# A two-block transformer on one core: squares of the pre-MLP norm added on VectorE, a third slot for split weights, and the last PSUM copies on ScalarE

## The reference, cut to what matters

```python
for l in range(DEPTH):                     # DEPTH = 2, D = 1024, D_FF = 4096, all float32
    h = rms_norm_2(x, pre_mix_w[l])
    u = h @ w_in[l]                        # in2_l
    ...                                    # convolution, attention, gated delta rule
    y = concat([y_conv, y_diff, y_delta]) @ w_out[l]          # out2_l
    x = x + rms_norm_2(y, post_mix_w[l])   # post-norm and
    h = rms_norm_2(x, pre_mlp_w[l])        # pre-norm, both at the start of ff1_l
    y = square(relu(h @ w_ff1[l])) @ w_ff2[l]                 # ff1_l, ff2_l
    x = x + rms_norm_2(y, post_mlp_w[l])
# rms_norm_2(x, w) = x * rsqrt(mean(x*x, over the 1024 channels) + 1e-6) * w
```

## Time and profile before

| what | value |
|---|---|
| median of 3 runs | 4168.87 us (4166.24 to 4171.51) |
| profiled execution, its own time | 4178.81 us |
| its span | 4177.0 us |
| PE busy | 3878.9 us, 93% |
| DVE busy | 2185.2 us, 52% |
| ACT busy | 1493.1 us, 36% |
| POOL busy | 343.9 us, 8% |

### The profile page before, as it was taken

The page is one execution under the profiler, slowest core; times in us unless marked ns, Lnnn a source line. Parts: engine busy times, 40 slices in busy tenths (PEclk is TensorE's granted clock), DMA queues, the critical chain, the costliest instruction groups (busy, mean ns, idle before and its releaser), DMA issues. The chain is left out here.

```text
span 4177.0 us, 49727 instructions
## 1 busy us (share of the span) xinstructions
PE 3878.9 (93%) x20585; PEld 3108.8 (74%) x20585; DVE 2185.2 (52%) x3124; ACT 1493.1 (36%) x2290; POOL 343.9 (8%) x296
## 2 busy tenths in 40 slices
PE   7997789999999999889999979989998979988998
PEld 4884667888888777678877757757786757866876
DVE  5725755555564332373256756543475846544375
ACT  2115632111453112152255335433364335533264
POOL 0000210000000000000000034300000025400000
PEclk9998989999999999999999979979999979988999
DMA  5510013343222111122323100022232200012231
GB/s 201 174 33 10 6 41 101 111 141 111 66 66 74 58 58 51 38 91 91 100 83 99 57 11 1 1 81 71 90 101 67 81 11 1 1 61 71 91 101 60
DMA packets 254720, 288.90 MB, mean 69 GB/s; under 512 B 6756, under 2 KB 226939, under 8 KB 254517
## 3 DMA queue, kind: packets, MB, share of 16 engines
q1 hardware_dynamic: 252437, 281.84, 20.9%
q10 hardware_dynamic: 2080, 4.19, 0.3%
HBM read 283.92 MB, written 2.10 MB: 68 GB/s over the span
## 5 line engine op out<-in xcount | busy, mean ns | idle before, releaser
L465 PE MATMUL banks<-h_halves,w_halves 128*128 128x512 f32 (+1 forms) x3728 | 1393.6, 374 | 60.0 <-DVE h_halves L259 42.3
L466 PE MATMUL banks<-h_halves,w_halves 128*128 128x512 f32 (+1 forms) x3728 | 1389.0, 373 | 0.0
L467 PE MATMUL banks<-h_halves,w_halves 128*128 128x512 f32 (+1 forms) x3728 | 1382.7, 371 | 0.0
L465 PEld LDWEIGHTS banks<-h_halves,w_halves 128*128 128x128 f32 x3728 | 714.9, 192 | 201.4 <-issue 49.1
L467 PEld LDWEIGHTS banks<-h_halves,w_halves 128*128 128x128 f32 x3728 | 712.4, 191 | 122.7
L466 PEld LDWEIGHTS banks<-h_halves,w_halves 128*128 128x128 f32 x3728 | 714.6, 192 | 118.4 <-issue 0.5
L259 DVE TENSOR_TENSOR w_halves<-work,w_halves 128x2048 fp32r<-128x2048 f32 (+1 forms) x215 | 488.3, 2271 | 466.5 <-ACT w_halves L254 466.3
L254 ACT ACTIVATE w_halves<-work 128x2048 fp32r<-128x2048 f32 (+1 forms) x215 | 407.3, 1894 | 524.8 <-PE banks L467 388.5
L254 ACT ACTIVATE h_halves<-kept 128x512 fp32r<-128x512 f32 (+1 forms) x520 | 332.3, 666 | 313.2 <-PE banks L467 234.0
L259 DVE TENSOR_TENSOR h_halves<-kept,h_halves 128x512 fp32r<-128x512 f32 (+1 forms) x520 | 361.4, 737 | 137.5 <-ACT h_halves L254 136.8
L990 DVE SCALAR_TENSOR_TENSOR kept<-kept 128x512 f32<-128x512 f32 x280 | 188.3, 746 | 7.4 <-DMA kept<-in_mod_w 7.4
(11 more groups left out here) (372 smaller groups left out, 4759.9 us busy)
## 6 DMA issues: line engine op xcount, KB each, us to landing
work<-in_w_ff SPq DMA_DIRECT2D x64, 1024.0 KB, 5.3
work<-in_ffn_w_in SPq DMA_DIRECT2D x44, 1024.0 KB, 5.1
kept<-in_mod_w SPq DMA_DIRECT2D x40, 1024.0 KB, 5.1
work<-in_odd_w_in SPq DMA_DIRECT2D x24, 1024.0 KB, 5.2
work<-in_w_in SPq DMA_DIRECT2D x24, 1024.0 KB, 5.0
work<-in_ffn_w_out SPq DMA_DIRECT2D x16, 1024.0 KB, 5.2
work<-in_even_w_in SPq DMA_DIRECT2D x13, 1024.0 KB, 5.2
work<-in_odd_w_out SPq DMA_DIRECT2D x8, 1024.0 KB, 5.3
```

The source lines that it names most:

```text
L465: nc.tensor.matmul(o, low[:, k - a, fc], rh[:, tc], start=(k == 0), stop=False)
L466: nc.tensor.matmul(o, high[:, k - a, fc], rl[:, tc], start=False, stop=False)
L467: mm = nc.tensor.matmul(o, high[:, k - a, fc], rh[:, tc], start=False, stop=(k == K - 1))
```

## The change

1. `PlainNorm` with `post`: the squares of x are no longer summed on TensorE tile by tile. `add_square` adds them on VectorE into `home.total`, each one behind the next tile's low half, and one set of `row_sums` (`squares_complete`) stands before the last tile of group 1.
2. A third pair of halves, `t_halves`. Where `third` is set (`up`, that is `ff1_l`, and `following`, that is `in2_1`) the stage before also splits unit 1, into it; the stage itself starts with two units split, and group 1 of the pair reads `t_halves`. The split of unit 1 in the norm is gone.
3. `CopySum`: in the last group ScalarE squares both banks and then copies both; VectorE only adds.

```diff
@@ PlainNorm
-        if self.post and g == 0:
-            for t in ([k - 1] if k else []) + ([k] if k == KD - 1 else []):
-                pe.wait_ge(self.squared, t + 1)
-                self.home.row_sums(self.nc, 7, self.home.sq[t % 2], t == 0, t == KD - 1).then_inc(self.sq_used, 1)
+    def squares_complete(self, pe):
+        pe.wait_ge(self.sq_used, KD)
+        self.home.row_sums(self.nc, 7, self.home.total).then_inc(self.summed, 1)
...
+    def add_square(self, dve, k):
+        if k == 0:
+            return
+        dve.wait_ge(self.squared, k + 1)
+        if k > 1:
+            dve.wait_ge(self.sq_used, k)
+        total = self.home.total
+        self.nc.vector.tensor_tensor(total, total if k > 1 else self.home.sq[0], self.home.sq[k % 2],
+                                     ALU.add).then_inc(self.sq_used, 1 if k > 1 else 2)
...
                 if k:
                     self.lower(dve, k - 1)
+                    self.add_square(dve, k - 1)
             self.lower(dve, KD - 1)
+            self.add_square(dve, KD - 1)
@@ Dense.run, two_groups
+                        if k == K + lag - 1:
+                            before.squares_complete(pe)
                         if k >= lag:
                             group_tile(1, k - lag)
-                    before.behind_groups(pe)
+                    before.back(pe)
@@ Dense.run, splitter
                 if self.started:
-                    eng.sem_inc(halves_done, 1)
+                    eng.sem_inc(halves_done, self.started)
...
-                    second(eng, (lambda: weights(0, 1)) if paired else None)
+                    second(eng)
...
-                if units > 1 and not paired:
+                if units > 1 and self.started < 2:
                     weights(0, 1)
@@ Dense.run, next_halves of ScalarE (VectorE's is alike)
                     after.first_high(act).then_inc(next_high, 1)
+                    if after.third:
+                        if fly:
+                            act.wait_ge(rhs_low, (G * C - 1) * KD)
+                        after.first_high(act, 1).then_inc(next_high, 1)
@@ CopySum
+            if n == KD - 2:
+                self.held = banks[0]
+            if n == KD - 1:
+                for m, bank in enumerate((self.held, banks[0])):
+                    nc.scalar.activation(core.sb(where(g, m) + CTX, SEQ), bank, ACT.Copy).then_inc(free, 1)
...
-            dve.wait_ge(self.sq_done, 2 * g + f + 1)
-            nc.vector.tensor_copy(core.sb(where(g, f) + CTX, SEQ), banks[0]).then_inc(free, 1)
+            if 2 * g + f < KD - 2:
+                dve.wait_ge(self.sq_done, 2 * g + f + 1)
+                nc.vector.tensor_copy(core.sb(where(g, f) + CTX, SEQ), banks[0]).then_inc(free, 1)
```

More of the change, by code:

```diff
@@ L278, in __init__ @@
         self.widths = widths or {}
-        self.base, self.retired, self.started = None, False, False
+        self.base, self.retired, self.started, self.third = None, False, 0, False
     def width(self, g):
@@ L299, in preload, with place, first_high, first_low @@
             self.load(sp, 0, u)
[L301 to L308, removed]
+    def place(self, u, low):
+        if u == 1 and self.third:
+            return self.core.t_halves[:, low * SLOT_W:(low + 1) * SLOT_W]
+        return self.core.half(u % SLOTS, low)
+    def first_high(self, act, u=0):
+        act.wait_ge(self.core.ring_ready[u], self.base[u] + 16)
+        self.started = u + 1
+        return halves_high(self.core, act, self.place(u, 0), self.core.sb(RING0 + u * SLOT_W, SLOT_W))
+    def first_low(self, dve, u=0):
+        return halves_low(self.core, dve, self.place(u, 1), self.core.sb(RING0 + u * SLOT_W, SLOT_W), self.place(u, 0))
     def run(self, name, after=None, before=None, side=None):
@@ L481, in group_tile @@
                         pe.wait_ge(low_done, j + 1)
-                    high, low = (core.half(j, n).rearrange("p (k n) -> p k n", k=KD) for n in range(2))
+                    high, low = (self.place(j, n).rearrange("p (k n) -> p k n", k=KD) for n in range(2))
                     if j == 0:
@@ L599, in next_halves @@
                     after.first_low(dve)
+                    if after.third:
+                        dve.wait_ge(next_high, 2)
+                        after.first_low(dve, 1)
                 first, second = (before.vector_first, before.vector) if before is not None else (None, None)
@@ L1133, in tensor, with scalar @@
         self.home.spread(self.nc, 0, places).then_inc(self.spread, 1)
-    def scalar(self, act, weights=None):
+    def scalar(self, act):
         core, nc = self.core, self.nc
@@ L1158, in lower, with vector @@
         ins.then_inc(self.low, 1)
-    def vector(self, dve, weights=None):
+    def vector(self, dve):
         core, nc = self.core, self.nc
@@ L1237, in after_tile, with back, scalar @@
     def after_tile(self, pe, g, k):
-        if self.post and g == 0:
-            for t in ([k - 1] if k else []) + ([k] if k == KD - 1 else []):
-                pe.wait_ge(self.squared, t + 1)
-                self.home.row_sums(self.nc, 7, self.home.sq[t % 2], t == 0, t == KD - 1).then_inc(self.sq_used, 1)
         if not self.post and (g, k) == (0, 4):
-            self.behind_groups(pe)
-    def behind_groups(self, pe):
+            self.back(pe)
+    def squares_complete(self, pe):
+        pe.wait_ge(self.sq_used, KD)
+        self.home.row_sums(self.nc, 7, self.home.total).then_inc(self.summed, 1)
+    def back(self, pe):
         pe.wait_ge(self.rstd_done, 1)
         self.home.spread(self.nc, 1, self.places(6)).then_inc(self.spread, 1)
-    def scalar(self, act, weights=None):
+    def scalar(self, act):
         core, nc = self.core, self.nc
@@ L1254, in scalar @@
             self.home.root(nc, 0, 5).then_inc(self.y_std, 1)
-            weights()
         for k in range(KD):
@@ L1268, in scalar @@
         if self.post:
-            act.wait_ge(self.sq_used, KD)
+            act.wait_ge(self.summed, 1)
             self.home.root(nc, 1, 7).then_inc(self.std_done, 1)
@@ L3408, in second_layer @@
     up = Dense(core, a["w_ff1_2"][l], core.h, KD, D_FF // GW, plain(0), lat, ScaledSquaredRelu(core, nc, U0))
+    up.third = True
     out.run(f"out2_{l}", after=up)
@@ L3413, in second_layer @@
                                                     (PV0 + ROW_POSTMIX + 8 * l, y_view)))
+    if following is not None:
+        following.third = True
     down.run(f"ff2_{l}", after=following)
```

1 line of the change is left out of this document (added).

## The result

The changed kernel takes 4139.42 us (median of 4 runs, 4136.52 to 4142.80), the kernel before 4167.56 (4 runs, 4165.21 to 4171.51): ratio 0.9927, 95% interval 0.9913 to 0.9941, or 28.1 us faster by the medians (30.4 by the ratio). The forecast was 4143.7, with a range of its own of 4139 to 4148.

A forecast was written before the change was run, and what follows sets the result against it. TensorE, 93% busy, was taken to bound the kernel. Per stage 0.91 + 1.0 + 8.2 - 1.9 - 0.15 = 8.06 us; three stages 24.2, plus 1.0 at the end: 4168.87 - 25.2 = 4143.7, own range 4139 to 4148, wider 4137 to 4152.

The forecast's parts named there:

- Third slot: Post-norm start of three stages: unit 1's split moves to the stage before, first y product sooner, gain 0.91 us a stage.
- Its cover: End of the stage before: the added split should finish before the last group's squares, 3.2 us ahead on VectorE in out2_0.
- Copies: End of all four CopySum stages: ScalarE copies both banks, VectorE only adds; gain 1.0 us each, bounds 0.4 to 1.2.
- Squares: Inside the pair: TensorE loses seven of eight sets of narrow row sums, gain 8.2 us a stage.
- Given back: Between the pair and group 2: later row sums delay the weights' split; 1.9 us a stage lost, TensorE idle about 4 us.
- Does VectorE keep up: Inside the pair: seven more VectorE adds, blocked by GpSimd's three, deliver just in time; charge 0.15 us a stage, bounds 0 and 3.
- the layout: Step-by-step VectorE schedule inside the pair, with GpSimd's blocking: when low halves arrive against when TensorE wants them.
- Restart: Start of group 2: TensorE already restarts at the low clock, so its longer idle is charged nothing more.
- Rival 2: Both starts of each stage: higher clock 6 products sooner without interrupting row sums, 2.4 us a stage more, 4136.5; 1 in 12.
- Rival 1: Inside the pair: VectorE starves TensorE, which waits 2 to 3 us a stage, 4151; 1 in 10.
- Rival 3: Inside the pair: short waits for low halves keep the clock at 1.2 GHz, 16.8 us a stage, 4194; 1 in 25.
- Rival 4: Stage before: unit 1's load lands late, squares queue behind its split, 1 to 2 us a stage lost, 4148; 1 in 14.

The follow-up runs named there:

- squares: The kernel before with only the squares added on VectorE and one set of row sums: 4149.28 us, ratio 0.9955.
- load: The changed kernel with a second, useless VectorE add of 0.60 us behind each added square: 4147.54 us, ratio 0.9961 to the kernel before.
- again: The kernel before, unchanged, run as a control: 4167.72 us, ratio 1.0004.
- early: The changed kernel with the row sums two tiles sooner and the spread ahead of the last tile: 4125.02 us, ratio 0.9890 to the kernel before.
- slot: The kernel before with only the third pair of halves, unit 1 split in the stage before: 4156.72 us, ratio 0.9970.
- shift1: The kernel before with a useless VectorE add of 128 x 3584 at the start of in2_0, outside the changed stages: 4171.36 us, ratio 1.0014.
- copies: The kernel before with only the last two CopySum copies moved to ScalarE: 4155.28 us, ratio 0.9967.
- border: The kernel before with the third pair of halves and ScalarE's copies together, squares still on TensorE: 4157.64 us, ratio 0.9974.
- earlynopool: The kernel early with GpSimd's three adds to x given to VectorE: 4129.21 us, ratio 0.9903 to the kernel before.
- nopool: The changed kernel with GpSimd's three adds to x given to VectorE: 4143.14 us, ratio 0.9936 to the kernel before.
- hold: The kernel early with a useless VectorE add between the spread and its copy, lengthening TensorE's idle: 4138.22 us, ratio 0.9929 to the kernel before.

## Why the prediction was right, and where it was short

The mechanism held, and the time lies inside the forecast's own range, 0.4 us above its lower end. Its terms for a stage, against the traces (means of three; the unchanged kernel's two profiled executions agree within 0.1 but for D):

- *Third slot*, 0.91: measured 0.90, alone and in the whole. Its cover held: between split and first square ScalarE idled 5.9, 6.6 and 5.9 us.
- *Copies*, 1.0: measured 1.01 to 1.02.
- *Squares*, 8.2: B fell by 8.50. Some 8.2 are the seven sets. The rest comes from the clock: 11, 8 and 11 products of the three pairs run slowly, where 12 each did, at 0.2 us a product. In the kernel squares B fell by 8.0, with 14, 13 and 12 slow ones.
- *Given back*, 1.9: measured 1.80. TensorE's idle there is 3.9 us, as said.
- *Does VectorE keep up*, 0.15: measured 0 in two stages and 0.2 in `in2_1`. VectorE itself waited 0.34 us ahead of low halves 3 and 5 (not 5 in `in2_1`), since ScalarE waits there for GpSimd's x. In `ff1_0` the low halves 3, 5 and 6 ended 0.6, 0.8 and 0.8 us before the first product that uses them, where the layout had 0.4, 0.1 and 0.1. load shows how near this is: 0.60 us a tile more, and TensorE waits 1.8 us a stage.
- *Restart*, charged 0, "so I charge nothing more for that": D is 13.28 and not 13.83 us (13.36 in again, where one stage was slow for a shorter time). Of group 2's first products 14, 13 and 14 ran slowly before and 11, 9 and 11 now. The clock is low for the same 6.83 us; before, then now, in `ff1_0`:

```profile
2849.98:2856.81 6.83, 6.17 (x15) 0.50 0.38 131
2832.75:2839.58 6.83, 5.14 (x12) 0.50 0.48 154
```

  Group 2 starts at 2850.64, 0.66 us into the stretch, and now at 2834.44, 1.69 us into it: more of it passes while TensorE waits. What the term left out is larger: with a shorter wait there is no low stretch at all (early, 11.01).
- *Not in the sum*: the row sums of y take 1.48, 1.03 and 1.48 us for 1.86, and so root and spread come sooner: 0.4 us in two stages, 0.8 in `in2_1`. They start 1.0 us sooner, and in `ff1_0` the clock falls only 0.44 us after their start, where it had fallen 0.74 us before it. The 0.8 is in part luck of the execution: slot, squares and shift1, whose row sums start no sooner, also took 1.03 in `in2_1`, and copies 1.68.

So a stage gains 9.7 us by these rows and not 8.06 (64.94 - 55.25), the final one 28.4 - 27.1 = 1.3: 30.4 in all. The two profiled executions differ by 42.0. The other 11.6 lie outside what the change touches, and again, the same kernel, shows what they are: its profiled execution took 4168.88 and not 4178.81, 6.5 of these 9.9 us before the first changed stage. Against it the four parts give 3 x 9.25 + 1.0 = 28.7, and the medians 28.1. The prediction was right to set its sum against the medians.

Rival 2 (more through the clock, 4136.5) had the right effect at too large a price, some 1.0 to 1.4 us a stage and not 2.4, and the wrong cause: in squares, where the row sums are gone too, no fewer products ran slowly. Rival 1: 0.60 us a tile more brings it on; how much less would do wasn't run, and tile 5 of `in2_1` already shows its first sign. Rival 3 has nothing for it: waits inside the pair left the clock high. Rival 4 had 5.9 us of room on ScalarE.

**Why the parts do not add.** The pair starts at the low clock, so a microsecond taken out ahead of it has no fixed price. Here is the stretch at 1.2 GHz around the pair's start in `ff1_0` (us, PE busy, PEclk, DMA share, GB/s): before, squares, copies, slot, border, after.

```profile
2802.19:2819.26 17.07, 9.80 (x31) 0.50 0.41 123
2795.85:2812.92 17.07, 10.04 (x30) 0.50 0.40 123
2799.09:2812.74 13.65, 7.12 (x24) 0.50 0.50 154
2793.26:2806.92 13.66, 7.46 (x24) 0.50 0.49 154
2797.56:2811.21 13.65, 8.02 (x26) 0.50 0.48 154
2795.21:2808.86 13.65, 8.02 (x26) 0.50 0.48 154
```

Counted from the first square, it ends at 19.8 us before and at 20.1 in squares, and at 16.6 in copies, in slot, in border and after (in `in2_1`, in the same order: 19.0, 18.8, 16.4, 15.5, 15.4, 15.1). In `ff1_0` either part alone ends it 3.2 us sooner, and the second adds nothing to that: it lets products start sooner that then run at half speed (slow products of the three pairs: 12, 12, 12 before, 9, 8, 6 in copies, 8, 7, 7 in slot, 12, 9, 12 in border). From the first square to the pair's last product (A + B) it is 47.53 us before, 45.40 with copies, 45.33 with slot, 44.64 with both: the first microsecond brings 2.2, the second 0.7. D goes the same way: 13.8 and 13.4 before, 12.1 and 12.6 with one part, 12.8 with both. In the whole, the border's two parts on top of squares bring 58.22 - 55.25 = 3.0 us a stage, 8.9 in three, and 0.9 at the end; the medians say 9.9.

Against again, a stage gains 3.4 us by copies, 3.0 by slot and 6.3 by squares, 12.7 in sum, and 9.25 in the whole. Copies and slot each claim some 2 us a stage of the clock beyond their own 1.0 and 0.9; the whole keeps 1.0. So the sum of 46.8 is too large by 3.4 us a stage, 10.2 of its 18.7, because it counts a share that comes only once. Squares has next to none of that share. The other 8.5 us show in no row of these stages and lie within what the times leave open.

The Trainium skill's page "SBUF — State Buffer", section "Who interferes with whom", was used as the reason for the charge at GpSimd's adds. The trace agrees that the two exclude each other for whole instructions: the first low half again took 1.67 us. But who waits is not always VectorE: at tiles 3 and 5 it was GpSimd in five of six cases (2.33 us for 1.26), at no cost to TensorE, and VectorE in the sixth (1.78 us for 0.68), where TensorE lost 0.2 us. The charge laid out by that rule was due in one stage of three.

**What stays open.** The rows of the three stages and the end give 11.2 us for copies (3 x 3.42 + 0.95) and 14.1 were measured; for slot 8.9 and 12.6; for border 11.4, and 10.0. What is left, 1 to 4 us of either sign, is within the intervals, and lies in stretches that these kernels leave alone; those took 3939 to 3954 us in the profiled executions. Why the low stretch around the pair's start ends some 3 us sooner with either part isn't shown, only that it does. Why a 2.1 us idle slows the restart in 19 of the 21 stages looked at and not in two, and 3.5 us in two of three, isn't settled either.

## What to carry to other kernels

Work that TensorE does for another engine between products was paid in full here, so moving it to an engine with room was the safe part of the change. Ask next what the last of it hangs on: moved two tiles forward, with the spread ahead of the last tile, the same row sums bring 14 us more than the change itself, since TensorE then idles 0.9 us before group 2 and not 3.9. And where a wait stands ahead of products at the low clock, test the parts together, since each alone claims the clock's share.

## What the runs showed of the hardware

- TensorE's wait ahead of group 2 and the granted clock behind it: 0.9 us left it at 2.4 GHz in 6 of 6 stages (early, earlynopool), 2.1 us lowered it to 1.2 GHz for part of the next products in 19 of 21, 3.9 us in 12 of 12 (after, squares, load, nopool). 3.5 us lowered it in 2 of 3 (hold). The price is D: 11.0 us for 48 products without a fall, 12.4 to 13.9 with one.
- Nine waits of 0.23 to 0.93 us inside the pairs of load left the clock high.
- With VectorE instructions queued back to back, a waiting GpSimd add let two of them pass in five of six cases of the changed kernel (2.33 us for 1.26) and one in the sixth (1.73 us), where the VectorE add behind took 1.78 us for 0.68.
- The stretch at 1.2 GHz around a pair's start in `ff1_0` lasted 17.07 us before and in squares, and 13.65 with copies, slot or both.
- The first profiled execution of the kernel before was 9.9 us longer than the second, in stretches that are the same in both.
